# Two transformer blocks on one core: the recurrence's triangular solve on 32×32 diagonal blocks, and the gating's layer norm moved into the attention rounds

## The reference, cut to what matters

```python
def step(state, inp):                      # RWKV-7, 8 heads of 64, state 64x64
    r_t, w_t, k_t, v_t, a_t, b_t = inp
    sa = einsum("bhvk,bhk->bhv", state, a_t)
    state = state * w_t + sa[..., None] * b_t + v_t[..., None] * k_t
    return state, einsum("bhvk,bhk->bhv", state, r_t)
...
def _chunked_spatial_gating(u, v, ln_g, ln_b, w_s, b_s):   # chunks of 128 tokens, 4 groups of 128
    vn = _layernorm(v, ln_g, ln_b).reshape(b, nc, CHUNK, N_GROUPS, GROUP_W)
    w = where(causal[None], w_s, 0)
    sv = einsum('gts,bnsgc->bntgc', w, vn) + b_s.T[None, None, :, :, None]
    return u * sv.reshape(b, s, D_B)
...
y_a = _swa_with_sinks(q, k, v, sinks) * silu(z_a)
y_b = _chunked_spatial_gating(gelu(u_b), gelu(v_b), ln_v_g, ln_v_b, w_s, b_s) * silu(z_b)
merged = sigmoid(g_a) * (y_a @ w_proj_a) + sigmoid(g_b) * (y_b @ w_proj_b)
```

## Time and profile before

| | |
|---|---|
| median of 3 runs | 1412.94 us (1411.88 to 1413.27) |
| the profiled execution | 1413.47 us, span of its instructions 1412.2 us |
| TensorE (PE) busy | 1393.5 us, 99% |
| VectorE (DVE) busy | 814.5 us, 58% |
| ScalarE (ACT) busy | 479.1 us, 34% |
| GpSimd (POOL) busy | 136.8 us, 10% |
| mean granted TensorE clock | 0.997 of full |

### The profile page before, as it was taken

The page is one execution under the profiler, slowest core; times in us unless marked ns, Lnnn a source line. Parts: engine busy times, 40 slices in busy tenths (PEclk is TensorE's granted clock), DMA queues, the critical chain, the costliest instruction groups (busy, mean ns, idle before and its releaser), DMA issues.

```text
span 1412.2 us, 20873 instructions
## 1 busy us (share of the span) xinstructions
PE 1393.5 (99%) x8982; PEld 1112.5 (79%) x8982; DVE 814.5 (58%) x1134; ACT 479.1 (34%) x723; POOL 136.8 (10%) x138
## 2 busy tenths in 40 slices
PE   7999999999999999999999999999999999999998
PEld 5687887878778888887778888887887877888886
DVE  7374654746548755354575674556635435767754
ACT  6332324234135333234431221323243232443323
POOL 1020302002002011001210000000040011003000
PEclk9999999999999999999999999999999999999999
DMA  5110201111042333322255543232221333212262
GB/s 190 59 46 32 76 32 60 47 46 61 32 164 90 105 120 119 105 75 75 90 179 194 194 164 101 93 97 93 86 100 65 98 97 104 90 61 75 79 174 90
DMA packets 42205, 136.18 MB, mean 96 GB/s; under 512 B 4650, under 2 KB 8362, under 8 KB 42113
## 3 DMA queue, kind: packets, MB, share of 16 engines
q1 hardware_dynamic: 33984, 114.57, 24.9%
q0 software_dynamic: 4080, 14.68, 2.8%
q10 hardware_dynamic: 4048, 5.59, 1.1%
HBM read 130.37 MB, written 2.10 MB: 94 GB/s over the span
## 4 chain that ended last, share of the span: by engine, by line
PE 95%; DVE 2%; DMA 1%; ACT 1%; issue 1%; ACTq 0%; DVEq 0%
PE bank L417 93%; PE bank L420 2%; DMA w_raw<-panels 1%; DVE opA_lo L1426 1%; DMA xT<-x 1%; DVE w_lo L1418 0%; DVE tmp L1426 0%; ACT scores L928 0%; DVE P L1426 0%; ACT w_hi L928 0%; DVE scores L1418 0%; ACT opA_hi L928 0%; DVE tmp L1418 0%; DVE x_tokens L1426 0%; DVE pad L1418 0%
## 5 line engine op out<-in xcount | busy, mean ns | idle before, releaser
L1418 DVE TENSOR_TENSOR w_lo<-w_raw,w_hi 128x1024 fp32r<-128x1024 f32 (+1 forms) x209 | 257.4, 1232 | 348.0 <-ACT w_hi L928 347.7
L417 PE MATMUL bank<-opA_hi,w_hi 128*128 128x512 f32 x1000 | 410.8, 411 | 10.2 <-DVE opA_lo L1426 8.2
L417 PE MATMUL bank<-opA_hi,w_lo 128*128 128x512 f32 x1000 | 395.7, 396 | 0.0
L417 PE MATMUL bank<-opA_lo,w_hi 128*128 128x512 f32 x1000 | 394.6, 396 | 0.0
L928 ACT ACTIVATE w_hi<-w_raw 128x1024 fp32r<-128x1024 f32 (+1 forms) x209 | 220.1, 1053 | 368.3 <-DMA w_raw<-panels 368.1
L417 PEld LDWEIGHTS bank<-opA_hi,w_hi 128*128 128x128 f32 x1000 | 188.1, 188 | 64.6 <-issue 16.4
L417 PEld LDWEIGHTS bank<-opA_hi,w_lo 128*128 128x128 f32 x1000 | 188.3, 188 | 45.6
L417 PEld LDWEIGHTS bank<-opA_lo,w_hi 128*128 128x128 f32 x1000 | 188.5, 189 | 41.6 <-issue 2.2
L417 PE MATMUL bank<-opB_hi,w_hi 128*128 128x512 f32 x448 | 178.5, 398 | 0.3 <-DVE w_lo L1418 0.3
L417 PE MATMUL bank<-opB_hi,w_lo 128*128 128x512 f32 x448 | 177.2, 395 | 0.0
L417 PE MATMUL bank<-opB_lo,w_hi 128*128 128x512 f32 x448 | 177.2, 395 | 0.0
(11 more groups left out here) (317 smaller groups left out, 1624.5 us busy)
## 6 DMA issues: line engine op xcount, KB each, us to landing
w_raw<-panels SPq DMA_DIRECT2D x208, 512.0 KB, 3.3
ada_w<-ada POOLq DMA_DIRECT2D x24, 512.0 KB, 4.5
xT<-x ACTq DMA_DIRECT2D x1, 2048.0 KB, 14.5
x_tokens<-x_blocks SPq DMA_DIRECT2D x16, 128.0 KB, 4.0
out<-x_tokens SPq DMA_DIRECT2D x8, 256.0 KB, 2.0
memT<-mem ACTq DMA_DIRECT2D x1, 1024.0 KB, 5.7
xT<-x ACTq DMA_DIRECT2D x3, 256.0 KB, 7.5
xT<-x SPq DMA_DIRECT2D x3, 256.0 KB, 7.3
```

The lines of the kernel that those rows point to most:

```text
L417: return pe.matmul(o, lhsT, rhs, start=start, stop=stop, skip_group_check=True)
L1418: return ve.tensor_tensor(o, a, b, op)
```

## The change

With B = 32, the levels 2 to 16 of the solve are done on the four diagonal 32×32 blocks of a chunk's pair of heads (`BLOCKS`), each with its own product; `X`, `Yt` and a new tile `XTb` hold the blocks alone, 32 columns a chunk. Level 32 makes only the one block off the diagonal, from the blocks, and VectorE copies it into `XT`. The straight A·B in bank 3 is made for the diagonal blocks alone. ScalarE copies the blocks of bank 4 to `XTb` at the start and those of `XTb` to `XT` behind level 16; GpSimd clears `XT` once at the start. The number of filler steps is the same.

In the second block the statistics of the layer norm move to the za/zb panels before the rounds, with the root; the norm is made by VectorE alone, two tiles in round 1 and two in round 2, behind the scaling of the scores. w_s is turned by TensorE in round 1 and masked by VectorE in round 2. The products w_s·vn and the gate row stand right behind round 3, ahead of all remaining 42 steps (`F2_LAST`); VectorE's gating groups are split by `F2_GATING` = 6 steps. GpSimd makes UB·ZB before the rounds. In the first attention the products with v go tile by tile, each waiting for its own copy.

```diff
@@ -571,11 +574,16 @@
 
             pe.wait_ge(ar_done, 2 * f + 2)
             pe.wait_ge(b2_done, f + 1)
-            for dst, left_, right in ((3, AR, BK), (4, BK, AR)):
-                for c in range(NC):
+            for c in range(NC):
+                for e in (0, B):
                     for lo, hi in HH:
-                        ins = mm(bank[dst][lo:hi, c * L:(c + 1) * L], left_[lo:hi, c, 0:L], right[lo:hi, c, 0:L])
-                ins.then_inc(ab_mm, 1)
+                        ins = mm(bank[3][lo + e:lo + e + B, c * B:(c + 1) * B], AR[lo:hi, c, e:e + B],
+                                 BK[lo:hi, c, e:e + B])
+            ins.then_inc(ab_mm, 1)
+            for c in range(NC):
+                for lo, hi in HH:
+                    ins = mm(bank[4][lo:hi, c * L:(c + 1) * L], BK[lo:hi, c, 0:L], AR[lo:hi, c, 0:L])
+            ins.then_inc(ab_mm, 1)
-            pe.wait_ge(abt_done, f + 1)
+            pe.wait_ge(xt_copied, 9 * f + 5)
...
-                        for lo, hi in HH:
-                            ins = mm(bank[2 + 2 * g][lo:hi, q * L:(q + 1) * L], ABT[lo:hi, c, :], X[lo:hi, c, :])
+                        if n < len(LEVELS) - 2:
+                            for lo, hi, e in BLOCKS:
+                                ins = mm(bank[2 + 2 * g][lo:hi, q * B:(q + 1) * B], ABT[lo:hi, c, e:e + B], X[lo:hi, c, :])
+                        else:
+                            for lo, hi in HH:
+                                ins = mm(bank[2 + 2 * g][lo + B:hi, q * B:(q + 1) * B], ABT[lo:lo + B, c, B:L],
+                                         X[lo:lo + B, c, :])
                     ins.then_inc(y_mm, 1)
...
-                            for lo, hi in HH:
+                            if last:
+                                for lo, hi in HH:
+                                    ins = mm(bank[6 + g][lo:lo + B, q * B:(q + 1) * B], Yt[lo + B:hi, c, :],
+                                             XTb[lo + B:hi, c, :])
+                                continue
+                            for lo, hi, _ in BLOCKS:
                                 if turned:
-                                    ins = mm(bank[6 + g][lo:hi, q * L:(q + 1) * L], Yt[lo:hi, c, :], XT[lo:hi, c, :])
+                                    ins = mm(bank[6 + g][lo:hi, q * B:(q + 1) * B], Yt[lo:hi, c, :], XTb[lo:hi, c, :])
                                 else:
-                                    ins = mm(bank[3 + 2 * g][lo:hi, q * L:(q + 1) * L], XT[lo:hi, c, :], Yt[lo:hi, c, :])
+                                    ins = mm(bank[3 + 2 * g][lo:hi, q * B:(q + 1) * B], XTb[lo:hi, c, :], Yt[lo:hi, c, :])
                         ins.then_inc(x_mm, 1)
...
-            pe.wait_ge(xt_level, 10 * f + 10)
+            pe.wait_ge(xt_level, 12 * f + 12)
+            pe.wait_ge(xt_copied, 9 * f + 9)
...
-            pe.wait_ge(pt_v, h + 1)
-            pe.wait_ge(pt_a, h + 1)
-            for mt in range(2):
-                evicted("kv", KT + 2 * h + mt)
             if h:
                 pe.wait_ge(op_lo, OPERAND["xo"] + 2 * h)
-            for d in range(2):
-                for mt in range(2):
+            for mt in range(2):
+                pe.wait_ge((pt_v, pt_a)[mt], h + 1)
+                evicted("kv", KT + 2 * h + mt)
+                for d in range(2):
                     c = h * XD + d * NP
                     ins = mm(bank[6 + d][:, :], vtm[:, mt, c:c + NP], pT[n][:, mt, :], mt == 0, mt == 1)
-                ins.then_inc(weigh_mm, 1)
+                    if mt:
+                        ins.then_inc(weigh_mm, 1)
...
+            if t == 1:
+                pe.wait_ge(gating_here, 64)
+                pe.wait_ge(sv_step, 1)
+                for g4 in range(4):
+                    ins = turn(bank[6][:, g4 * NP:(g4 + 1) * NP], wsr[:, g4, :])
+                ins.then_inc(ws_mm, 1)
...
+            if t == 2:
+                pe.wait_ge(ws_done, 1)
...
-        pe.wait_ge(gating_here, 64)
-        pe.wait_ge(op_lo, OPERAND["merge2"] + 3)
-        for g in range(4):
-            ins = turn(bank[6][:, g * NP:(g + 1) * NP], wsr[:, g, :])
-        ins.then_inc(ws_mm, 1)
-        p.steps(F2_MID)
         pe.wait_ge(vn_v, 4)
-        pe.wait_ge(vn_g, 4)
-        pe.wait_ge(ws_done, 1)
         for g in range(4):
             for n in range(4):
                 ins = mm(bank[2 + g][:, n * NP:(n + 1) * NP], vn[:, n, g * NP:(g + 1) * NP], wst[:, g, :])
             ins.then_inc(sv_mm, 1)
-        p.steps(F2_LAST)
-        pe.wait_ge(ws_done, 1)
         pe.wait_ge(sv_step, 4)
...
+        p.steps(F2_LAST)
...
-            act(ABT[:, :, :], c8(bank[4][:, :]), ACT.Copy).then_inc(abt_done, 1)
+            act(ABT[:, :, :], c8(bank[4][:, :]), ACT.Copy).then_inc(xt_copied, 1)
+            for lo, hi, e in BLOCKS:
+                act(XTb[lo:hi, :, :], c8(bank[4][:, :])[lo:hi, :, e:e + B], ACT.Copy).then_inc(xt_copied, 1)
...
-            p.steps(5 * F_SOLVE + F_Z)
+            p.steps(4 * F_SOLVE)
+            ac.wait_ge(xt_level, 12 * f + 8)
+            if f == 0:
+                ac.wait_ge(ones, 2)
+            for lo, hi, e in BLOCKS:
+                act(XT[lo:hi, :, e:e + B], XTb[lo:hi, :, :], ACT.Copy).then_inc(xt_copied, 1)
+            p.steps(F_SOLVE + F_Z)
...
+        gp.wait_ge(lora_mm, 3 * FT)
+        gp.memset(XT[:, :, :], 0.0).then_inc(ones, 1)
...
-            gp.wait_ge(abt_done, f + 1)
-            tt(XT[:, :, :], ABT[:, :, :], wide("level1_turned", NC), ALU.mult).then_inc(xt_done, 1)
+            gp.wait_ge(xt_copied, 9 * f + 5)
+            tt(XTb[:, :, :], XTb[:, :, :], wide("level1_turned", NC), ALU.mult).then_inc(xt_done, 1)
             gp.wait_ge(xt_done, 2 * f + 1)
-            tt(XT[:, :, :], XT[:, :, :], wide("eye", NC), ALU.add).then_inc(xt_done, 1)
+            tt(XTb[:, :, :], XTb[:, :, :], wide("eye", NC), ALU.add).then_inc(xt_done, 1)
...
+        for g in range(4):
+            i = FIRST["zb"] + g
+            gp.wait_ge(left[i % 2], left_after(i))
+            tt(P[:, UB + g, :], P[:, UB + g, :], P[:, ZB + g, :], ALU.mult).then_inc(uz_done, 1)
...
-                    tt(Yt[:, 4 * g:4 * g + 4, :], bank[2 + 2 * g][:, 0:4 * L].rearrange("p (c l) -> p c l", c=4),
-                       wide(f"level{s}", 4), ALU.mult).then_inc(y_done, 1)
+                    ps = bank[2 + 2 * g][:, 0:4 * B].rearrange("p (c l) -> p c l", c=4)
+                    if last:
+                        ve.tensor_copy(Yt[:, 4 * g:4 * g + 4, :], ps).then_inc(y_done, 1)
+                    else:
+                        tt(Yt[:, 4 * g:4 * g + 4, :], ps, wide(f"level{s}", 4), ALU.mult).then_inc(y_done, 1)
...
+                        o, b = (XTb, 6 + g) if turned else (X, 3 + 2 * g)
+                        ps = bank[b][:, 0:4 * B].rearrange("p (c l) -> p c l", c=4)
+                        if last:
+                            for lo, hi in HH:
+                                ve.tensor_copy(XT[lo:lo + B, d, B:L], ps[lo:lo + B]).then_inc(xt_level, 1)
+                        else:
+                            tt(o[:, d, :], o[:, d, :], ps, ALU.add).then_inc(xt_level if turned else x_level, 1)
...
+        for n in range(4):
+            ve.wait_ge(vb_made, n + 1)
+            ve.bn_stats(st6[:, n, :], vn[:, n, :]).then_inc(bn_step, 1)
+            ve.wait_ge(bn_step, 2 * n + 1)
+            ve.bn_aggr(mv[:, n, :], st6[:, n, :]).then_inc(bn_step, 1)
+            if n == 1:
+                p.steps(KT)
+        ve.wait_ge(bn_step, 8)
+        ts(mv[:, :, 1:2], mv[:, :, 1:2], 1.0, ALU.mult, EPS, ALU.add).then_inc(bn_step, 1)
         p.to("gates2")
 
         p.steps(2)
         mx, nm, su, rs = (stat2[:, 8 * q:8 * q + 8] for q in range(4))
+        ve.wait_ge(root_done, 5)
+        ve.reciprocal(mv[:, :, 1:2], mv[:, :, 1:2]).then_inc(bn_step, 1)
+
+        def value_norm(n):
+            ve.wait_ge(bn_step, 10 + n)
+            ve.wait_ge(gating_here, 64)
+            stt(vn[:, n, :], vn[:, n, :], mv[:, n, 0:1], lng[:, :], ALU.subtract, ALU.mult).then_inc(bn_step, 1)
+            ve.wait_ge(bn_step, 10 + n + 1)
+            stt(vn[:, n, :], vn[:, n, :], mv[:, n, 1:2], lnb[:, :], ALU.mult, ALU.add).then_inc(vn_v, 1)
...
+            if t == 2:
+                ve.wait_ge(ws_mm, 1)
+                tt(wst[:, :, :], bank[6][:, :].rearrange("p (g t) -> p g t", g=4), wide("causal", 4),
+                   ALU.mult).then_inc(ws_done, 1)
+            if t in (1, 2):
+                value_norm(2 * t - 2)
+                value_norm(2 * t - 1)
             p.steps(F2_SOFTMAX)
             if t:
...
-        p.steps(F2_LAST)
+            if g == 1:
+                p.steps(F2_GATING)
         ve.wait_ge(ws_mm, 2)
         for b in range(2):
             ve.tensor_copy(gate_row[:, b * S:(b + 1) * S], bank[6 + b][:, :]).then_inc(ws_done, 1)
+        p.steps(F2_LAST - F2_GATING)
```

More of the change, by code:

```diff
@@ L45 @@
 LEVELS = [1, 2, 4, 8, 16, 32]
+B = L // 2
 MATS = [("ident", 128), ("mean", 128), ("head_sum", 128), ("cumsum", 128), ("chunk_mask", 128),
```

(32 more changed lines are left out.)

65 lines of the change are left out of this document (15 added, 50 removed).

## The result

The changed kernel takes 1445.69 us (median of 6 runs, 1437.95 to 1451.31) against 1412.36 for the kernel before in the same series: ratio 1.0229, interval 1.0199 to 1.0258. It is 33 us slower by the medians, 2.3% by the ratio; the forecast was 21.6 us faster.

A forecast was written before the change was run, and what follows sets the result against it. TensorE, busy 99% of the span, was taken to bound the kernel. From the median 1412.94 us, solve −25.2, gating +3.9 and first attention −0.3 gave −21.6, so 1391.3 us; range 1385 to 1416.

The forecast's parts named there:

- the cost of a level: Solve: TensorE's time for one level falls from 3.84 to 2.58 us, with no waits for other engines costed.
- Rival (2): Solve levels: program supply runs dry in part, 9 to 14 ns a matmul, 1394 to 1411, say 1402 us; chance 0.14.
- the clock sentence at the end: Whole kernel: clock stays 9 in all slices; if smaller tiles let it fall, the prediction is wrong as a whole.
- Rival (1): New solve: instructions, not columns, bind; 1465 us at 29 ns a matmul, 1432 at 20 ns; chance 0.16.
- The sets: Solve: each set takes 0.51 us instead of 0.93; 15 sets in each of four f, 25.2 us less.
- The line over columns: Solve: a pair's time grows with columns streamed, 0.8 ns a column plus about 0.007 us, so 32 columns take 32 ns.
- Four tiles at once, levels' dependency, copies on ScalarE and GpSimd at nothing: Solve: four tiles run together; the dependency of 1.6 us fits inside 2.58; the other engines' copies stay hidden; all cost zero.
- Rival (3): Solve: only two tiles run at once, a full set takes 1.02 us, 1418 us in all; chance 0.06.
- Gating rounds: Second attention: norm operations on VectorE delay queued work; TensorE waits 2.9 us more in round 1, 1.9 in round 2.
- The old wait of 0.91 at the w_s products: Second attention: TensorE's wait for GpSimd's last v_norm operation before w_s·v_norm goes away, −0.9 us.
- Head 3's wait of the first attention: First attention: TensorE's 0.73 us wait for ScalarE's probs_t copy becomes one for VectorE's, 0.3 us earlier: −0.3.
- The rule of 60 cycles: Solve: the skill's overhead per matmul, so small dimensions should not be tiled; as a floor over all tiles, forbids this change.

The follow-up runs named there:

- bursts: Kernel before plus 2304 products on constants, in five shapes, ahead of the first recurrence's A·B products; ran once, 1547.83 us against 1412.59.
- halved: Kernel before with each 64×64 product of the five solve levels issued as two of 32 moving columns; 1465.7 us, ratio 1.0379.
- spread_all: Kernel before with only the solve changed, four filler steps a level laid between the sets, two in the last level; 1411.04 us, ratio 0.9988.
- gating_alone: Kernel before with only the change's gating and first-attention parts, solve as before; 1416.87 us, ratio 1.0033.

## Why the prediction was wrong, step by step

**The step that failed** is the cost of a level: 2.58 us of TensorE's own work, with the supply of program at nothing in the sum. Rival (2) held that term, at the wrong size, and with it fell the clock sentence at the end. The prediction saw that one piece of program would be drawn in 2 us, and priced a dry supply at 9 to 14 ns a matmul. No row that it had showed how fast pieces can come: its 5.7 us was the rate at which the kernel before drew them. The bursts show 27 to 31 ns. The piece comes every 3.45 to 4.0 us, so the 195 matmuls of a level want 5.3 us at the least, where the level had 3.84 before and was to have 2.58. Rival (1) named the right number, 29 ns "the densest sustained rate", and asked whether it was the engine's limit: for a burst it is not (9.4 ns), on average over more than one piece it is. Its 1465 us took each set by itself at that rate, and left out that filler steps, few matmuls in a long time, make up for part of it.

**The 32 us, in terms.** (a) The sets: 64 matmuls in 0.60 us for 32 in 0.93, 15 sets, four recurrences: about −20. The prediction had 0.51 and −25.2. The line over columns behind it was wrong (halved), and came within 0.1 us of the set by chance. (b) TensorE idle: +31. Of it 25.9 are the 18 stops in the solves, 1.1 is a wait for VectorE's eviction of P ahead of the second recurrence's levels that the kernel before does not have, and the gating half has 3.7 by its own page (busy 1393.0, span 1415.4). (c) The lower clock: the mean granted clock is 0.981 against 0.997; busy time rose by 0.9 although the sets saved 20, so 21 us went to slower work. With the same matmuls in spread_all, clock 0.998, busy time is 1383.0: −20 + 9.3 of changes between shapes gives −10.7, measured −10.5. (c) is a remainder in the changed kernel. The windows with the clock at 0.50 or 0.51 bear it out; their sums, of nine stretches in the changed kernel and of one (1059.6 to 1066.4 us) before:

```profile
sum 54.60, PE 50.50; mean PE 5.61
sum 6.80, PE 6.80; mean PE 6.80
```

TensorE did 50.5 us of work at the lower clock where it did 6.8 before. Were all of it half as long at full clock, that is (50.5 − 6.8)/2 = 21.9 us, an upper estimate: on the small tiles of the bursts the lower clock costs a factor of 1.6 only (13.3 ns a matmul for 8.5). That the stops bring the lower clock was not tried by itself; where they shrank to 5.6 us, in spread_all, it was gone from the solves.

**Four tiles at once, levels' dependency, copies on ScalarE and GpSimd at nothing:** right. Rival (3) is refuted by 9.4 ns a matmul. No stop in the levels has VectorE, ScalarE or GpSimd as its releaser; VectorE held TensorE once, for the 1.1 us ahead of them.

**"Clock stays 9; if smaller tiles let it fall, the prediction is wrong as a whole":** it fell, in three slices, but behind the stops. Two windows of bursts (columns as above), the first in the burst of 32 columns, the second mostly in that of 64 on the same small tiles:

```profile
108.00:124.00 16.00, 9.30 (x515) 8.74 (x512) 0.00 (x0) 0.00 (x0) 0.00 (x0) 0.50 0.02 4
...
195.00:222.00 27.00, 15.58 (x900) 14.37 (x896) 0.00 (x0) 0.00 (x0) 0.00 (x0) 0.94 0.02 4
```

TensorE was busy 58% of either, with stops of 1.5 to 1.8 us in the one and mostly 1.2 to 2.0 in the other, and the clock was low in the one and nearly full in the other. The two shares are not the same work: the first is already stretched by the low clock, at which 128 matmuls take 1.93 us, where 161 took 1.55 at full clock. Both run on the same small tiles, so these alone do not decide it; what does was not settled.

**Gating rounds:** mechanism right, size nearly. Round 1: 3.72 us of waiting for 3.3; and then, in the changed kernel, 16 transposes took 3.56 us instead of 1.91 at a lower clock, which the prediction did not have (+1.6); in the profile of gating_alone the wait was 3.41 and the transposes took 1.91. Round 2: 1.22 and 0.21 us for 1.9, the first behind the eviction of P and not the copy of probs_t. The old wait of 0.91 at the w_s products is gone, as said. Head 3's wait of the first attention fell from 0.73 to 0.43, as said:

```profile
671.61 2.81 PE L420 MATMUL bank<-probs_t,v_mem 128*128 128x512 f32 x6 [0.43 <-issue]
```

Sum: forecast +3.6 with the first attention's 0.3. The waits of gating_alone's profile give 3.0 + 1.2 + 0.2 − 0.9 − 0.3 = +3.2, as its span does (1415.4 for 1412.2); measured over all runs +4.7.

**The rule of 60 cycles.** The overhead of about 60 cycles a matmul (the Trainium skill, "TensorEngine Tiling (Array Packing)", section Instruction Overhead) was given 0.16. As a floor over all tiles it is refuted by 9.4 ns a matmul; on one tile the only shape run, 128 × 16 with 16 moving columns, took 25.0 ns. Its advice, not to tile a dimension that is already small, was right for this kernel, for another reason.

**Open.** Of the 3.45 to 4.0 us of a piece the transfer itself is only 1.1 (the queue's 1.8% of 16 engines over 34 us are 9.8 us for nine pieces); what the 1.0 to 1.7 us ahead of it and the 1.2 to 1.6 behind it go to was not settled. Nor was it settled how far ahead the next piece is asked for: behind the slower 64 × 64 burst 289 matmuls of 128 × 16 at 25.0 ns ran without a stop, over two of the places where a piece ends. That spread_all stays at 1411 is explained by its terms, not tried apart from them.

## What to carry to other kernels

Count TensorE's instructions by 128 matmuls, as the trace counts them (a float32 product is two), and compare each stretch of them with 3.45 to 4.0 us: under that, smaller or faster matmuls bought idle time here, and a lower clock came with it. A solve is made cheaper by narrowing products whose count does not rise, as in the last level, or by long matmuls among the short ones, which costs 0.29 us a change here and left 1.7 us of gain (spread_all, by the ratio). And when work moves to an engine with time to spare, look at what is queued right behind it: putting two pairs of operations behind two copies, in place of in front of them, turned 4.7 us of loss into 1.7 of gain (by the ratios).

## What the hardware showed that was not expected

Stops with no releaser, exactly 128 matmuls apart in the bursts, on every tile shape faster than 27 ns a matmul, and each ending 1.2 to 1.6 us behind the landing of a 16 KB packet on the queue q8. The 59 ns of a pair of 64-column weights with 32 as with 64 moving columns. From start to start, 9.4 ns a matmul on four tiles of 32 × 32 × 32 in the kernel (8.5 in the first burst), at most 19 ns on two of them (0.62 us for 32 with a change to filler), 15.9 ns on two tiles of 64 × 32, 25.0 ns on one tile of 128 × 16. The 0.29 us for a change from filler to small tiles and back. And a first burst of 161 matmuls in 1.55 us without a stop, ahead of the first one: more than one piece's worth, as fits one whole piece in reserve, which was not tried by itself.
